# The second attention of a two-block transformer kernel: from single query tiles, tokens by features, to pairs of query tiles, features by tokens

## The reference, cut to what matters

```python
def blocked_bidirectional_attention(q, k, v):      # 8 heads, 1024 queries, 1024 keys
    def one_block(q_blk):
        s = jnp.einsum('bqhd,bkhd->bhqk', q_blk, k).astype(jnp.float32) * scale
        p = jax.nn.softmax(s, axis=-1).astype(v.dtype)
        return jnp.einsum('bhqk,bkhd->bqhd', p, v)
...
    o_attn = blocked_bidirectional_attention(q, k, v) * jax.nn.silu(g_attn)
...
    y = r_attn * (o_attn @ w_br_attn) + r_conv * (o_conv @ w_br_conv) + r_mem * (o_mem @ w_br_mem)
    return x + y @ w_out
```

## Time and profile before

| | |
|---|---|
| Time, median of 3 runs | 2874.79 us (2872.86 to 2876.85) |
| Time of the profiled execution | 2877.45 us |
| Its span from first to last instruction | 2875.7 us |
| PE busy | 2737.6 us, 95% of the span |
| DVE, ACT, POOL busy | 48%, 24%, 33% |
| Share of PE in the chain that ended last | 87% |
| Mean granted clock of PE | 0.975 of full |
| The second attention in the trace | from about 1695 to 1962 us |

### The profile page before, as it was taken

How to read it: one execution, slowest core, us unless ns; L and a number is a source line. 1 busy time by engine, 2 the same in 40 slices (tenths; PEclk the granted TensorE clock), 3 DMA queues, 4 the chain that set the end, 5 groups by cost and what they waited for, 6 DMA issues and landing times.

```text
span 2875.7 us, 34919 instructions
## 1 busy us (share of the span) xinstructions
PE 2737.6 (95%) x14088; PEld 2236.7 (78%) x14088; DVE 1374.4 (48%) x1494; ACT 701.9 (24%) x972; POOL 939.2 (33%) x443
## 2 busy tenths in 40 slices
PE   6999799998899999999979989999999999989899
PEld 3888577776688888888867769998888878778777
DVE  4726888864544444544456656662002321342331
ACT  4200133333312121111234444442000020141010
POOL 1434422202254443434423300003343433523333
PEclk8999799999899999999989999999999999999999
DMA  5111222221111111111121100001111111112112
GB/s 236 37 44 52 69 76 71 66 103 41 37 47 49 51 44 44 52 50 51 44 95 45 37 8 1 1 1 37 52 59 52 46 42 52 59 45 103 44 37 88
DMA packets 36673, 155.88 MB, mean 54 GB/s; under 512 B 4164, under 2 KB 4296, under 8 KB 35016
## 3 DMA queue, kind: packets, MB, share of 16 engines
q1 hardware_dynamic: 33264, 127.04, 13.5%
q10 hardware_dynamic: 1528, 20.71, 1.8%
q0 software_dynamic: 1760, 6.36, 0.9%
HBM read 145.70 MB, written 8.39 MB: 54 GB/s over the span
## 4 chain that ended last, share of the span: by engine, by line
PE 87%; DVE 8%; DMA 1%; ACT 1%; issue 1%; POOL 1%; DVEq 0%; ACTq 0%; POOLq 0%; SPq 0%
PE region L265 22%; PE region L267 21%; PE region L266 21%; PE pv L696 8%; PE aux L684 4%; DVE conv L820 3%; PE region L796 2%; PE pv L342 1%; PE region L798 1%; DVE tmp L418 1%; PE aux L351 1%; PE pv L506 1%; DVE h_lo L412 1%; DMA rs_again<-rs_spill 1%; DVE x L1597 1%
## 5 line engine op out<-in xcount | busy, mean ns | idle before, releaser
L1655 POOL TENSOR_TENSOR w_hi<-w_raw,der 128x1024 fp32r<-128x1024 f32 x186 | 360.6, 1939 | 1696.0 <-PE region L267 1650.7
L265 PE MATMUL region<-h_hi,w_hi 128*128 128x512 f32 x1760 | 694.3, 394 | 44.3 <-DVE h_lo L412 21.4
L267 PE MATMUL region<-h_hi,w_lo 128*128 128x512 f32 x1760 | 689.5, 392 | 0.0
L266 PE MATMUL region<-h_lo,w_hi 128*128 128x512 f32 x1760 | 689.4, 392 | 0.0
L1658 POOL TENSOR_TENSOR w_lo<-w_raw,w_hi 128x1024 fp32r<-128x1024 f32 x186 | 498.3, 2679 | 14.6
L265 PEld LDWEIGHTS region<-h_hi,w_hi 128*128 128x128 f32 x1760 | 333.4, 189 | 123.0 <-issue 48.3
L267 PEld LDWEIGHTS region<-h_hi,w_lo 128*128 128x128 f32 x1760 | 333.1, 189 | 70.4
L266 PEld LDWEIGHTS region<-h_lo,w_hi 128*128 128x128 f32 x1760 | 333.6, 190 | 68.4
L265 PE MATMUL region<-ff_hi,w_hi 128*128 128x512 f32 x512 | 199.2, 389 | 0.0
L266 PE MATMUL region<-ff_lo,w_hi 128*128 128x512 f32 x512 | 199.2, 389 | 0.0
L267 PE MATMUL region<-ff_hi,w_lo 128*128 128x512 f32 x512 | 199.2, 389 | 0.0
(11 more groups left out here) (317 smaller groups left out, 4091.1 us busy)
## 6 DMA issues: line engine op xcount, KB each, us to landing
w_raw<-units SPq DMA_DIRECT2D x186, 512.0 KB, 3.6
w_raw<-w_ada_late SPq DMA_DIRECT2D x32, 512.0 KB, 3.6
ada_buf<-w_ada SPq DMA_DIRECT2D x4, 2048.0 KB, 13.8
toep<-rpb_pad POOLq DMA_DIRECT2D x16, 288.0 KB, 5.8
x_sb<-x_t ACTq DMA_DIRECT2D x2, 2048.0 KB, 14.3
x<-x_t ACTq DMA_DIRECT2D x1, 4096.0 KB, 13.0
x_spill<-x ACTq DMA_DIRECT2D x1, 4096.0 KB, 11.8
x<-x_spill ACTq DMA_DIRECT2D x1, 4096.0 KB, 14.3
```

What stands on the lines that cost most here:

```text
L265: pe.matmul(dst, wh, xh, start=first, stop=False)
L266: pe.matmul(dst, wh, xl, start=False, stop=False)
L267: return pe.matmul(dst, wl, xh, start=False, stop=last)
L1655: pool.tensor_tensor(w_hi[:, s], w_raw[:, s], one_col.broadcast_to([P, 1024]), ALU.mult)\
```

## The change

`mla` no longer uses the common class `Attention`; it has functions of its own, over 32 pairs i of query tiles, with s = 0 or 1 for the tile in the pair. What differs:

- **The values** have `v2` as weights (128 keys by 64 features of the one head) and `prob_t` as moving data (128 queries). The two tiles of a pair write to partitions 0 to 63 and 64 to 127 of `pv`, alternately for each of eight key blocks. The result is features by tokens, and the two tiles share an accumulation buffer. There are 16 such matmuls in a pair, as many as before.
- **The normalization** can no longer be done after the values, where a query is now a column. DVE multiplies `prob` (128x1024) by the reciprocal of the row sum, in place, before the transposes (`norm`), and frees the region at its start. After the values, `store` is two plain copies of 64x128 into `o_heads`, features by tokens, for the pair.
- **The eviction** of all transposes is ACT's: four copies of 128x512 in a pair instead of two by ACT and two by DVE. `aux` is handed over by halves.
- **The orders.** PE: scores(i,0), values(i-2), turn(i-1,0), scores(i,1), turn(i-1,1). ACT: exps(i,0), move(i-1,0) in two halves, exps(i,1), move(i-1,1) in two halves. DVE: maxes(i,0), norm(i,0), store(i-2), maxes(i,1), norm(i,1). The splits for the next head are spread out, one ACT copy behind exps(i,0) in each of two pairs of a head, and one DVE subtraction behind norm(i,1) in each of two.
- **The waits.** exps(i,s) waits for the transposes of tile (i-1,s), whose buffer `prob[:, s]` it overwrites. values(i) waits for all four moves of its pair. A move waits for the values of the pair before, whose `prob_t` it overwrites.
- **The gate stage** of `mla` has no transposes and no wait for the stores on PE; DVE reads `o_heads` directly.

```diff
-    mla = Attention("mla", HEADS, T, (prob, prob_t), mla_score,
-                    lambda i, b: v2[:, b, P * (i // TT // 2):P * (i // TT // 2) + P], head_store(o_tok2),
-                    ahead_act=mla_act_ahead, ahead_dve=mla_dve_ahead)
+    MLA_N = HEADS * TT // 2
+    def mla_pe(e, pos):
...
+        def turn(i, s):
+            reach(e, "mla_prob", 2 * i + s + 1)
+            for half in range(2):
+                if s or i:
+                    reach(e, "mla_pt", 4 * i + 2 * s + half - 1)
+                for b in range(4 * half, 4 * half + 4):
+                    last = e.transpose(aux[:, b * P:(b + 1) * P], prob[:, s, b * P:(b + 1) * P], ident[:])
+                last.then_inc(sem("mla_turned"), 1)
+
+        def values(i):
+            h = i // 4
+            reach(e, "mla_pt", 4 * i + 4)
+            if i >= 2:
+                reach(e, "mla_stored", i - 1)
+            for b in range(TT):
+                for s in range(2):
+                    last = e.matmul(pv[64 * s:64 * s + 64, i % 2, 0:P], v2[:, b, 64 * h:64 * h + 64], prob_t[:, s, b],
+                                    start=(b == 0), stop=(b == TT - 1))
+                    if b == TT - 1:
+                        last.then_inc(sem("mla_summed"), 1)
+
+        for i in range(MLA_N + 2):
+            for s in range(2):
+                if i < MLA_N:
+                    scores(i, s)
+                if s == 0 and i >= 2:
+                    values(i - 2)
+                if 1 <= i < MLA_N + 1:
+                    turn(i - 1, s)
+
+    def mla_act(e, pos, ch):
...
+        def exps(i, s):
+            m = 2 * i + s
+            reach(e, "mla_maxed", m + 1)
+            if i:
+                reach(e, "mla_turned", 2 * (m - 1))
+            e.activation(prob[:, s], region[:, s], ACT.Exp, bias=neg_max[:, m % 4:m % 4 + 1],
+                         accum_out=row_sum[:, m % 4:m % 4 + 1]).then_inc(sem("mla_exp"), 1)
+
+        def move(i, s, half):
+            reach(e, "mla_turned", 2 * (2 * i + s) + half + 1)
+            if i:
+                reach(e, "mla_summed", 2 * i)
+            copy(e, prob_t[:, s, 4 * half:4 * half + 4], aux[:, half * HALF:half * HALF + HALF].rearrange("p (b k) -> p b k", k=P))\
+                .then_inc(sem("mla_pt"), 1)
...
+        for i in range(MLA_N + 1):
+            for s in range(2):
+                if i < MLA_N:
+                    exps(i, s)
...
+                if i:
+                    move(i - 1, s, 0)
+                    move(i - 1, s, 1)
+
+    def mla_dve(e, pos, ch):
...
+        def norm(i, s):
+            m = 2 * i + s
+            reach(e, "mla_exp", m + 1)
+            e.sem_inc(free[s], 1)
+            ch(e.reciprocal(inv_sum[:, m % 4:m % 4 + 1], row_sum[:, m % 4:m % 4 + 1]))
+            e.tensor_scalar(prob[:, s], prob[:, s], inv_sum[:, m % 4:m % 4 + 1], None, ALU.mult).then_inc(sem("mla_prob"), 1)
+
+        def store(i):
+            h = i // 4
+            rows = slice(64 * (h % 2), 64 * (h % 2) + 64)
+            reach(e, "mla_summed", 2 * i + 2)
+            for s in range(2):
+                t = 2 * (i % 4) + s
+                last = e.tensor_copy(o_heads[rows, h // 2, t * P:(t + 1) * P], pv[64 * s:64 * s + 64, i % 2, 0:P])
...
+        for i in range(MLA_N + 2):
+            if i < MLA_N:
+                maxes(i, 0)
+                norm(i, 0)
+            if i >= 2:
+                store(i - 2)
+            if i < MLA_N:
+                maxes(i, 1)
+                norm(i, 1)
...
-            reach(pe, "mla_stored", HEADS * TT)
-            gate_pe(pe, pos, "ga", "gattn", o_tok2)
+            gate_pe(pe, pos, "ga", "gattn", None)
```

More of the change, by code:

```diff
@@ L87 @@
     "norm": [("n1", 8), ("nc", 8), ("lnn", 4), ("n2", 8), ("n3", 8), ("nq", 3), ("nk", 2), ("nm", 8)],
-    "att": [("na", 64), ("mla", 64), ("ma", 32)],
+    "att": [("na", 64), ("ma", 32)],
     "gate": [("ga", 4), ("gm", 4)],
@@ L92 @@
 SHARED = {tag: (kind, stages[:i]) for kind, stages in KINDS.items() for i, (tag, _) in enumerate(stages)}
-COUNTS = {f"{tag}_{what}": 1 for tag, _ in KINDS["rms"] for what in ("root", "rs")} | {f"br{b}_part": 4 for b in range(3)}
+COUNTS = {f"{tag}_{what}": 1 for tag, _ in KINDS["rms"] for what in ("root", "rs")} | {f"br{b}_part": 4 for b in range(3)} | {"ga_tb": 0}
 def build(nc, x_t, ctx_t, mem_t, w_ada, w_ada_late, units, small, rope_c, rope_s, rpb_pad, mask, positions, out, x_spill,
@@ L189, in build @@
     pos_i = nc.alloc_sbuf_tensor_at("pos_i", [P, T], I32, offset=arena + 160 * 1024)
-    o_tok2 = place("o_tok2", [TT, HALF], 144)
+    o_heads = place("o_heads", [4, T], 144)
     o_hi = place("o_hi", [4, T], 0, F32R)
@@ L1368, in build @@
     k_lo = place("k_lo", [HEADS, T], 64, F32R)
[L1370 to L1384, removed]
@@ L1386, in mla_low @@
-    def mla_low(e, h):
-        for n, (full, high, low) in enumerate([(q_h, q_hi, q_lo), (k_h, k_hi, k_lo)]):
-            reach(e, "qk_hi", 2 * h + n + 1)
[L1389 to L1401, removed]
@@ L1403, in build, with scores @@
-    mla = Attention("mla", HEADS, T, (prob, prob_t), mla_score,
-                    lambda i, b: v2[:, b, P * (i // TT // 2):P * (i // TT // 2) + P], head_store(o_tok2),
-                    ahead_act=mla_act_ahead, ahead_dve=mla_dve_ahead)
+    MLA_N = HEADS * TT // 2
+    def mla_pe(e, pos):
+        assert pos.use % 2 == 0
+        uses = {}
+        def scores(i, s):
+            h, t = i // 4, 2 * (i % 4) + s
+            use = uses[i, s] = pos.next_use()
+            if t == 0:
+                reach(e, "qk_lo", 2 * h + 2)
+            wait_region(e, use)
+            qs = slice(t * P, (t + 1) * P)
+            for lo in (0, HALF):
+                ks = slice(lo, lo + HALF)
+                last = mm3(e, region[:, s, ks], q_hi[:, h % 2, qs], q_lo[:, h, qs], k_hi[:, h % 2, ks], k_lo[:, h, ks], True, True)
+            last.then_inc(sem("mla_scored"), 1)
+        def turn(i, s):
[25 more added lines that the diff above has]
+                    turn(i - 1, s)
@@ new lines, in mla_act, with hi @@
+    def mla_act(e, pos, ch):
+        def hi(h, full, high):
+            if h >= 2:
+                reach(e, "mla_scored", TT * (h - 1))
+            copy(e, high[:, h % 2], full[:, h]).then_inc(sem("qk_hi"), 1)
+        def exps(i, s):
[11 more added lines that the diff above has]
+                .then_inc(sem("mla_pt"), 1)
+        hi(0, q_h, q_hi)
+        hi(0, k_h, k_hi)
+        for i in range(MLA_N + 1):
+            for s in range(2):
+                if i < MLA_N:
+                    exps(i, s)
+                    h = i // 4 + 1
+                    if s == 0 and i % 4 == 0 and h < HEADS:
+                        hi(h, q_h, q_hi)
+                    if s == 0 and i % 4 == 1 and h < HEADS:
+                        hi(h, k_h, k_hi)
+                if i:
+                    move(i - 1, s, 0)
+                    move(i - 1, s, 1)
+        pos.use += 2 * MLA_N
@@ new lines, in mla_dve, with low, maxes @@
+    def mla_dve(e, pos, ch):
+        def low(h, n):
+            full, high, below = ((q_h, q_hi, q_lo), (k_h, k_hi, k_lo))[n]
+            reach(e, "qk_hi", 2 * h + n + 1)
+            e.tensor_tensor(below[:, h], full[:, h], high[:, h % 2].bitcast(F32), ALU.subtract).then_inc(sem("qk_lo"), 1)
+        def maxes(i, s):
+            m = 2 * i + s
+            reach(e, "mla_scored", m + 1)
+            if m >= 4:
+                reach(e, "mla_exp", m - 3)
+            e.tensor_reduce(neg_max[:, m % 4:m % 4 + 1], region[:, s], AX, ALU.max, negate=True).then_inc(sem("mla_maxed"), 1)
+        def norm(i, s):
+            m = 2 * i + s
+            reach(e, "mla_exp", m + 1)
[9 more added lines that the diff above has]
+                last = e.tensor_copy(o_heads[rows, h // 2, t * P:(t + 1) * P], pv[64 * s:64 * s + 64, i % 2, 0:P])
+                if s:
+                    last.then_inc(sem("mla_stored"), 1)
+                else:
+                    ch(last)
+        low(0, 0)
+        low(0, 1)
+        for i in range(MLA_N + 2):
[7 more added lines that the diff above has]
+                norm(i, 1)
+                h = i // 4 + 1
+                if i % 4 == 1 and h < HEADS:
+                    low(h, 0)
+                if i % 4 == 2 and h < HEADS:
+                    low(h, 1)
+        reach(e, "mla_stored", MLA_N)
+        pos.use += 2 * MLA_N
@@ L1411, in gate_pe @@
         for j in range(4):
[L1412 to L1416, removed]
+            if src:
+                if j >= 2:
+                    reach(e, f"{tag}_gated", j - 1)
+                for t in range(TT):
+                    last = e.transpose(turned[j % 2][:, t * P:(t + 1) * P], src[:, t, j * P:(j + 1) * P], ident[:])
+                last.then_inc(sem(f"{tag}_tb"), 1)
             use = pos.next_use()
@@ L1428, in gate_act, with gate_dve @@
             copy(e, o_hi[:, j], tmp[:, 2 + j % 2]).then_inc(sem(f"{tag}_hi"), 1)
-    def gate_dve(e, pos, ch, tag):
+    def gate_dve(e, pos, ch, tag, src=None):
         for j in range(4):
```

(16 more changed lines are left out.)

## The result

The changed kernel takes 2934.39 us (median of 4 runs, 2931.59 to 2934.86), 2.05% more than before: ratio 1.0205, 95% interval 1.0188 to 1.0223; the kernel before, run beside it, took 2874.64. The profiled execution took 2934.72 us, 57.3 more than the one of before. The forecast was 2924.

A forecast was written before the change was run, and what follows sets the result against it. PE bounded the kernel before; after the change a closed ring of hand-overs, 9.61 us a pair against 8.11, would. With +51.3 at the gate's first projection and -2.6 in the gate stage, +48.7 us: 2924, range 2895 to 2985.

The forecast's parts named there:

- The ring: Closed path per pair through exp, scaling, store, maximum, second exp, moves, values, transposes: a floor of 9.61 us, against 8.11 before.
- values with wake-up and step back: PE's part of the period: waking PE 0.28, values 1.79, return from narrow to full-width matmuls 0.20 us.
- the head's copies: ACT's copies behind the first exp make the second exp 0.2 us late, 12 times from pair 4 on: 2.4 us.
- The clock: Rival, 12%: PE idles some 2 us each period, values and transposes run at 1.2 GHz, period grows 2.7 us: 3006 us.
- my case: Main forecast for the whole kernel: the closed path of hand-overs sets the period; 62%, range of its own 2905 to 2945 us.
- Beginning and end: Attention's fill and drain: exp(2,0) at 1719.1, exp(31,0) at 2000.2, the gate's first projection at 2014.9 us.
- my tail: After exp(31,0): transposes end 9.57 us later, then 0.64 + 0.6 + 0.7 + 0.6 + 2.1, PE through at about 2014.8.
- My +51.3: Forecast delay in us of the gate's first projection, from 1963.56 before to 2014.9 after.
- The values at half cost: Values matmuls to two disjoint partition halves run at once: 1.79 us a pair instead of 3.58, bounds 1.14 and 3.58.
- Values without overlap: Rival, 12%: the narrow values matmuls do not run at once, values stay 3.58 us, period 11.4 us: 2979 us.
- a shorter ring: Rival, 7%: faster values, no step back, scaling of 0.75 and quick hand-overs give a period of 8.7 us: 2895 us.
- PE as the bound: Rival, 5%: successive pairs overlap, the period is PE's own 6.5 us: 2820 us, faster than before.

The follow-up runs named there:

- e1: Changed kernel plus six matmuls of unread output in each pair from pair 2 on, put in PE's idle gap before the values: 2921.67 us.
- e5: Changed kernel with eviction shared again, ACT copying the first half of each turned tile and DVE the second: 2904.10 us.
- e2: Changed kernel with the values matmuls of a pair issued eight for one half of the partitions, then eight for the other: 2976.74 us.
- e7: Changed kernel with a third prob buffer and changed orders on ACT and DVE, so no engine waits ahead of ready work: 2825.03 us.
- e6: Changed kernel with only a third prob buffer, so the exp waits for the transposes of three tiles ago instead of two: 2888.60 us.
- e8: Changed kernel with changed orders on ACT and DVE, but still its two prob buffers: 2848.77 us.
- e4: Changed kernel with one extra 128x1024 DVE copy of unread output in each pair, between norm(i,0) and maxes(i,1): 2949.60 us.

## Why the prediction was right, and by what it missed

The direction and the cause held: slower, because a closed ring of hand-overs took PE's place as the bound. The forecast was +49 us and the measured change +60. The number came nearer than its terms: a ring summed 5.9 us too long hid a part of what the clock added. Step by step:

- **The ring** was forecast at 9.61 us and is 9.42 in even heads and 9.56 in odd ones. Term by term, forecast and then chain: exp and sum's read 1.20 and 1.21; to DVE 0.10 and 0.13; reciprocal 0.20 and 0.20; scaling with store 1.23 and 1.30 (1832.67 to 1833.97); maximum 1.27 and 1.26; second exp with two moves 2.43 and 2.19, since the copies start as soon as the sum is read, without the 0.12 gap that I took; values with wake-up and step back 2.27 and 2.01; transposes 0.91 and 1.12 with the hand-over. A further loss that I had put down, 0.2 us twelve times for the head's copies, did not happen. Those copies did something else: they delay the second half of `turn(i-1,1)` and so cut PE's idle time in two, 1.48 us ahead of these transposes and 1.10 ahead of the values (at 1824.48 and 1828.04), where a pair without them has 0.56 and 2.05 (at 1812.49 and 1816.99). Of these 29 periods the clock fell only in ones without the copies. Over 29 periods the forecast was 281.1 us; without clock falls they take 275.2 (e1): 5.9 too much.
- **The clock** is the term that was mis-sized. I kept it out of my case and gave it 12% as all or nothing, with 2.7 us in every period. It fell in 8 of 29, at 1.6 us each, 287.9 - 275.2 = 12.7 us. I called 2 us the safe side, because a gap of 2.35 us had passed without a fall. Three gaps were too few to read: in the same trace of before the clock fell behind one of 1.96 us (and again behind one of 2.19, at 2547.64). The gap, and a window behind it with the granted clock (0.50):

```profile
2460.98 0.50 PE L265 MATMUL region<-h_hi,w_hi 128*128 128x512 f32 x1 [1.96 <-POOL w_lo L1658]
```

```profile
2462.00:2463.00 1.00, 1.00 (x4) 0.50 0.73 205
```

  So the trace of before gave no ground to price this term at nothing. e1 showed cause and size, e5 that gaps up to 1.7 us did no harm.
- **Beginning and end.** exp(2,0) came 17.0 us behind the first exp instead of 16.3; from exp(31,0) to the gate's first projection it took 15.5 us instead of 14.7, with one more clock fall (values(30) 3.52 us). Together +1.5. The five terms of my tail add up to 2014.4 and not to the 2014.8 that I wrote; without that slip the difference would be 1.9.
- **The sum.** First exp to first gate projection took 260.8 us before (1702.76 to 1963.56) and 320.4 after (1703.55 to 2023.93): +59.6. My +51.3, -5.9, +12.7 and +1.5 make the same +59.6. The gate stage gave 2.5 back, forecast 2.6.
- **The values at half cost** came out, in part by luck: 3.58 us a pair before, 1.97 now, forecast 1.79 with 0.20 for the step back. Of the 1.61 saved, e2 puts 1.36 down to the alternation (3.33 to 1.97, which is 0.59 of the cost and not half); the other 0.25 is there without overlap, which the forecast did not have.
- **Rivals.** Values without overlap and a shorter ring did not come. PE as the bound did not come in this kernel, and e7 shows what that rival was worth: 2825 us, where it gave 2820. What kept it away was not the buffer's wait alone (e6), but that and the orders (e8, e7).

## What to carry to other kernels

Before moving work off the engine that bounds a loop, follow the program orders and waits once round: if exp, scaling, eviction and the next matmuls form a closed path, its length is a floor for the period, however idle each engine is. To get the gain, cut that path by a buffer and by orders in which no engine waits ahead of ready work; here either alone left another ring, 7.92 us with the buffer and 7.31 with the orders, against PE's 6.58 with both. And price what PE's idle gaps do to its clock as a share of the periods, not as all or nothing, after a look at every gap of that length in the trace and not at a few.

## What the runs showed of the hardware that was not expected

- A gap of about 2 us ahead of the values does not bring the clock down each time. With 2.04 to 2.17 us it fell in 8 periods of 17; with 0.6 us more (e4: 2.64 to 2.76 us) in 6 of 17; in e6, where only one pair in a head has such a gap, in 7 of 7. With gaps of 0.6 to 1.8 us (the other 12 periods of the changed kernel and of e4, and all of e5) it fell in none. The longer gap ahead of `values(30)`, 2.65 us in e6 and 3.56 in the changed kernel, brought it down in both. So for these gaps of 2.0 to 2.8 us the length alone does not settle it, and what else does stays open here.
- One idle stretch divided into two did no harm where the whole did: 1.48 and 1.10 to 1.24 us (12 periods, no fall) against about 0.55 and 2.04 to 2.17 (17 periods, 8 falls).
- In odd heads the ring is 0.13 us longer. There the scaling and the first store copy do not overlap. The timelines of DVE, an even head and an odd one:

```profile
1832.67 0.75 DVE L1473 TENSOR_SCALAR prob<-prob,der 128x1024 f32<-128x1024 f32 x1
1833.34 0.60 DVE L1481 COPY o_heads<-pv 64x128 f32<-64x128 f32 x2
```

```profile
1864.43 0.75 DVE L1473 TENSOR_SCALAR prob<-prob,der 128x1024 f32<-128x1024 f32 x1
1865.22 0.61 DVE L1481 COPY o_heads<-pv 64x128 f32<-64x128 f32 x2
```

  From scaling to copy it is 0.67 us in one and 0.79 in the other. In odd heads that copy goes from partitions 0 to 63 to partitions 64 to 127; whether that is the reason was not tried.
